# Moving the view of the activations that the up stages and the queries stream from to another offset from the weights

## The reference, cut to what matters

```
x = first_block(x, ...)     # attention, then an MLP
    h2 = rmsnorm(x, g_mlp)
    u  = relu(h2 @ w_up)                    # 2048 -> 8192
    x  = x + (u * u) @ w_down               # 8192 -> 2048
x = second_block(x, ...)    # two recurrent mixers, then PEER
    qry  = xn @ w_query                     # 2048 -> 2048
    hid  = gelu(u_tab[e] . xn);  y = sum gate * hid * v_tab[e]
                                # 16384 experts, 16 per head picked out of them
```

## Time and profile before

| what | value |
|---|---|
| time, median of 2 runs | 3207.76 us (3207.61 to 3207.91) |
| the profiled execution | 3207.3 us |
| its span, first to last instruction | 3205.3 us |
| granted clock of TensorE, mean over the span | 0.999 |
| TensorE busy | 3187.0 us |
| VectorE, ScalarE, GpSimd busy | 2030.2, 1447.6, 496.9 us |
| read from and written to HBM | 606.31 and 35.66 MB |

### The profile page before, as it was taken

The page is one execution under the profiler, slowest core; times in us unless marked ns, Lnnn a source line. Parts: engine busy times, 40 slices in busy tenths (PEclk is TensorE's granted clock), DMA queues, the critical chain, the costliest instruction groups (busy, mean ns, idle before and its releaser), DMA issues.

```text
span 3205.3 us, 48201 instructions
## 1 busy us (share of the span) xinstructions
PE 3187.0 (99%) x19975; PEld 2864.7 (89%) x19975; DVE 2030.2 (63%) x1837; ACT 1447.6 (45%) x1271; POOL 496.9 (16%) x418
## 2 busy tenths in 40 slices
PE   8999999999999999999999999999999999999999
PEld 7888899999999888888989999999999888888887
DVE  5455665555555667766466888999974555555554
ACT  5454453334343464464444444555543443343343
POOL 0000000000000002226300001988840000000000
PEclk9999999999999999999999999999999999999999
DMA  7444465555555443343256565677676666566563
GB/s 288 162 161 163 173 225 185 193 186 192 188 187 192 171 164 131 126 161 115 93 184 221 199 215 215 233 247 243 241 262 248 237 255 247 225 249 249 227 269 119
DMA packets 129572, 644.18 MB, mean 201 GB/s; under 512 B 12672, under 2 KB 45840, under 8 KB 60304
## 3 DMA queue, kind: packets, MB, share of 16 engines
q1 hardware_dynamic: 95792, 623.03, 53.5%
q10 hardware_dynamic: 33632, 18.99, 1.9%
HBM read 606.31 MB, written 35.66 MB: 200 GB/s over the span
## 4 chain that ended last, share of the span: by engine, by line
PE 97%; DVE 1%; ACT 1%; DMA 0%; SPq 0%; issue 0%; DVEq 0%; ACTq 0%
PE pj L313 12%; PE pj L314 12%; PE pj L315 12%; PE pj L289 7%; PE pj L290 7%; PE pj L291 7%; PE pj L1786 4%; PE pj L1788 4%; PE pj L904 4%; PE pj L1787 4%; PE pj L906 4%; PE pj L905 4%; PE pm L290 2%; PE pt L290 2%; PE pt L291 2%; PE pm L291 2%
## 5 line engine op out<-in xcount | busy, mean ns | idle before, releaser
L271 ACT ACTIVATE hi<-raw 128x2048 fp32r<-128x2048 f32 x534 | 1023.8, 1917 | 1374.1 <-PE pj L315 653.2
L278 DVE TENSOR_TENSOR lo<-raw,hi 128x2048 fp32r<-128x2048 f32 x400 | 918.2, 2296 | 679.8 <-ACT hi L271 679.2
L313 PE MATMUL pj<-xh_up,hi 128*128 128x256 f32 x3328 | 925.1, 278 | 0.0
L314 PE MATMUL pj<-xl_up,hi 128*128 128x256 f32 x3328 | 924.1, 278 | 0.0
L315 PE MATMUL pj<-xh_up,lo 128*128 128x256 f32 x3328 | 924.1, 278 | 0.0
L315 PEld LDWEIGHTS pj<-xh_up,lo 128*128 128x128 f32 x3328 | 628.8, 189 | 0.0
L314 PEld LDWEIGHTS pj<-xl_up,hi 128*128 128x128 f32 x3328 | 625.1, 188 | 0.6
L313 PEld LDWEIGHTS pj<-xh_up,hi 128*128 128x128 f32 x3328 | 624.9, 188 | 0.5
L278 DVE TENSOR_TENSOR lo_in<-raw,hi 128x2048 fp32r<-128x2048 f32 x134 | 308.3, 2301 | 267.6 <-ACT hi L271 266.8
L2509 POOL TENSOR_SCALAR hotA<-cst,slotT 128x128 fp32r<-128x128 f32 x256 | 338.1, 1336 | 460.9 <-ACT slotT L2347 424.5
L1786 PE MATMUL pj<-hi,xh_tok 128*128 128x512 f32 x576 | 231.2, 401 | 0.0
(11 more groups left out here) (412 smaller groups left out, 4239.0 us busy)
## 6 DMA issues: line engine op xcount, KB each, us to landing
raw<-w_peer SPq DMA_DIRECT2D x256, 1024.0 KB, 6.3
raw<-w_mlp SPq DMA_DIRECT2D x128, 1024.0 KB, 4.8
raw<-w_in SPq DMA_DIRECT2D x102, 1024.0 KB, 4.9
raw<-w_out SPq DMA_DIRECT2D x32, 1024.0 KB, 4.9
raw<-w_q SPq DMA_DIRECT2D x16, 1024.0 KB, 5.2
act_scratch<-hidU SPq DMA_DIRECT2D x32, 512.0 KB, 3.0
gates_scratch<-stage ACTq DMA_DIRECT2D x8, 2048.0 KB, 17.7
hidV<-act_scratch SPq DMA_DIRECT2D x32, 512.0 KB, 3.7
```

What stands on the lines that cost most here:

```text
L271: nc.scalar.activation(hi[:, j, :], raw[:, j, :], ACT.Copy).then_inc(hi_ready, 1)
L278: nc.vector.tensor_tensor(low(q)[:, j, :], raw[:, j, :], hi[:, j, :].bitcast(F32), ALU.subtract).then_inc(lo_ready, 1)
L313: nc.tensor.matmul(o, hi[:, j, cols], xh_up[:, k0 + k, :], start=clears, stop=False, skip_group_check=True)
L314: nc.tensor.matmul(o, hi[:, j, cols], xl_up[:, k0 + k, :], start=False, stop=False, skip_group_check=True)
```

## The change

The two views that are streamed in the up stages and the queries get an explicit address 192 bytes behind the one that they had, which is 384 bytes (mod 512) from the weights. The space that the tiles take stays the same: each of the two regions is still 16 KB and 512 bytes long, and everything behind them stays where it was. No instruction is added, taken away or moved; the instructions that write or read the two views do so at the new address.

```diff
+UP_SHIFT = 192
 TOK_SHIFT = 64
 COEF_REST = (0, 256)
...
         at_x = cursor[0]
-        xh_up = sb("xh_up", [P, KT, TT * P], F32R)
+        xh_up = sb("xh_up", [P, KT, TT * P], F32R, at=at_x + UP_SHIFT)
         xh_tok = sb("xh_tok", [P, KT, TT * P], F32R, at=at_x + TOK_SHIFT)
-        cursor[0] += 512
-        at_xl = cursor[0]
-        xl_up = sb("xl_up", [P, KT, TT * P], F32R)
+        at_xl = at_x + 4 * KT * TT * P + 512
+        xl_up = sb("xl_up", [P, KT, TT * P], F32R, at=at_xl + UP_SHIFT)
         xl_tok = sb("xl_tok", [P, KT, TT * P], F32R, at=at_xl + TOK_SHIFT)
-        cursor[0] += 512
+        cursor[0] = at_xl + 4 * KT * TT * P + 512
         at_y = cursor[0]
```

## The result

| kernel | time, median | spread of the runs |
|---|---|---|
| before | 3207.76 us | 3207.61 to 3207.91 |
| changed | 3253.73 us | 3253.66 to 3253.81 |

The ratio is 1.0143 (95% interval 1.0127 to 1.016): 46 us slower, within 2% but on the other side of the forecast, and 14 us above the upper end of the range. The profiled execution has a span of 3251.7 us against 3205.3 (granted clock, as a share of full speed, 0.999 in both).

A forecast was written before the change was run, and what follows sets the result against it. TensorE, busy 99%, was taken as the bound: matmul count times distance between starts. Removing the slow pace saves 12.0 us in 14 up stages plus 0.6, sum 12.7: 3207.8 - 12.7 = 3195.1 us; range 3192 to 3240.

The forecast's parts named there:

- What bounds the kernel: TensorE, busy 99% of the span: time is the number of matmuls times the distance between their starts.
- the parts costed at nothing: The 32 ACT and 32 DVE lifts, the feed by DMA, and the matmuls outside the up stages: no cost expected.
- So the change is worth what it makes of 4.5 ns: Per up matmul, 9984 in all, only the gap between paces of 113.33 and 117.8 ns was at stake.
- The price from the other side: If the slow pace spread to the 7152 clean up matmuls, 4.48 ns each, the loss would be 32.0 us.
- The likeliest case: Up stages: the slow pace does not hold at 384, all clean, 12.7 us saved, 3195.1 us; chance 0.42.
- The rows with 16 and 8 weight columns: Line 622: almost nothing read beside the stream, yet four first gaps of 117.5 ns, then 114; taken as evidence against.
- Rival 3: Queries and experts, 6912 matmuls, enter the slow pace at 384: 3239.8 us if all slow, otherwise 3226; chance 0.20.
- Rival 4: All 9984 up matmuls: both reads collide throughout, a worse overlap; 121.0 ns each needed for +2% (64 us); chance 0.08.
- Rival 2: Up stages: paces come from stage entry, or the slow one holds at 384 too; 3207.8 us, within 1; chance 0.27.
- Rival 5: Up matmuls faster than clean: 113.33 is itself a collision, loads alone leave 111.3 ns, 3175 us; chance 0.03.
- What would make it wrong: The entry into a stage chooses the pace, so the offset only re-deals which stages are slow; no size given.
- the 12.7 us: Saving if the slow pace goes: 12.0 us in 14 feed-forward up stages, 0.6 us in the first slow stretch.

The follow-up runs named there:

- the displaced kernel: Everything up to the activations starts 192 bytes later, streamed views keep the changed kernel's address, so their distance to the weights is 192; 3237.78 us (1.0094).

## Why the prediction was wrong

- **What bounds the kernel** held: TensorE is busy 99%, the price is read from start to start, and each ns per up matmul reached the end. So did the parts costed at nothing: lifts, feed and the other matmuls moved the time by under 3 us.
- **"So the change is worth what it makes of 4.5 ns"** is the step that failed first. It took the two paces seen at distance 192, 113.33 and 117.8 ns, for the only two that any distance has, and so the range priced a slow matmul at 4.5 ns. 384 has paces of its own, 118.7 and 120.0, and of these no clean one. The price from the other side, 7152 x 4.48 = 32.0 us, was no bound: it took the nearest row as the worst. With what was measured, the expert stage pays 33.0 us for 6144 (5.4 each), the queries 4.0, and the stretches that were slow already pay 2.2 more per matmul.
- **The likeliest case** (slow pace gone, 0.42) rested on the wide stages, which settle at 0 and 256. That was a false analogy. At the same 0 and 256 the narrow up matmuls are at their slowest of the eight distances, 120.0 ns. The wide ones have one load for twice the columns; that this gives them time for it is likely, but not shown. The rows with 16 and 8 weight columns, which I read as evidence against the loads, don't contradict them: little is loaded beside the stream, and from the fifth matmul on the gaps are 113 to 114 ns. Why the four before are slow stays open.
- **Rival 3** (the other side, 0.20) had the right sign and place: the clean experts lose it. It gave 3239.8 at most; measured 3253.73. The missing 14 us are the size of the excess: 5.3 to 6.7 instead of 4.5.
- **Rival 4** came nearest in mechanism (both reads collide throughout) and was held down by "no steady stretch in the trace has over 4.5", once more the trace of one distance taken for all of them.
- **Rival 2**, no effect: the runs speak against it. The same instructions take 3207.8 and 3262.1 us by where the streamed view lies, and at 256 halving the loads takes half or all of the excess away.
- **Rival 5**, a price below 113.33: no distance of the eight gave one.
- **What would make it wrong** was named rightly in part: the entry picks the pace at 192, as the displaced kernel and the coefficients show. But that explains the 12.7 us that I wanted to save, not the 46 that were lost.

## What to carry to other kernels

Where narrow matmuls (256 columns) with a full load of weights each run back to back, the place of the stream against the weights is worth up to 6% of their time (113.3 against 120.0 ns); scan it in steps of 32 bytes over a period of 256 before the layout is fixed, and measure each stage's distance from start to start. A pace that one layout shows is no bound for another layout (117.8 ns was the slowest at 192, 120.0 at 256), and wide matmuls say little on narrow ones: with the loads at 0 and 256 from the stream, the wide ones took 226.7 ns for 512 columns and the narrow ones 120.0 for 256. Where two steady paces exist, a stage can inherit the slow one from the stage in front (22.62 us here, and 21.79 with the loads of the down stage moved): look at its last loads. Moving only a part of them cost more here than moving all: with both parts of the coefficients at 192 the time was 3199.04 us, with the lo part alone 3202.15.

## What the runs showed of the hardware

- Loads and stream of TensorE aren't independent: with 256 columns streamed and 128 loaded, the gap is 113.3 to 120.0 ns by the distance in bytes between the loaded weights and the streamed view. It repeats after 256 bytes in the two pairs that were run (3261.45 and 3262.11 us at 0 and 256, 3207.4 and 3207.67 at 192 and 448). I had expected 0 to be harmless and a period of 512.
- At one distance two paces are steady, 113.3 and 117.8 ns, over as many as 1776 matmuls, and a stage shows within its first gaps which of them it has (in the displaced kernel 201, 120, 116, 116, 114 before the one and 201, 118, 118, 117, 119 before the other).
- Mixed distances in one train are no mean of the two: 3264.70 us with xh_up alone at 384, more than the 3253.73 with both there. In the wide down stages too: 226.7 ns at 0 and 256, 228.9 at 192, 231.0 with the lo part alone at 192.
- After a wait of 9.2 us TensorE ran 12 wide matmuls at a granted clock of 0.50, most 427 ns apart instead of 227 (the run with `row_pe` later).
- Why 192 (with 448) is the best of the eight, and why its neighbours at 32 bytes have a mixture of gaps, stays open: start times alone don't show it.
